# Two projection tiles with 16 extra columns: passes of 512 and 16 columns against passes of 256 and 272

## What is computed

```python
h = concatenate([zeros(PAD), meta, x])            # 16 meta tokens ahead of 512 tokens
hn = rms_norm_2(h, attn_norm_g)
proj = hn @ w_in
aq, ak, av, bq, bkv, iq, ik, iw, gates = split(proj, IN_SPLITS_2)
o_a = sliding_window_sink_attention(aq, ak, av, sinks, bias_a)   # ak: 2 key heads of 64, sliding branch
q = rms_norm_2(bq, q_norm_g) @ w_uq
c_kv = rms_norm_2(bkv, kv_norm_g)                 # 128 shared latent keys and values
o_b = indexed_sparse_mla(q_abs, c_kv, iq, layer_norm(ik), iw, w_uv, bias_b)
mixed = sigmoid(gate_a) * (o_a @ w_branch_a) + sigmoid(gate_b) * (o_b @ w_branch_b)
h = h + mixed @ w_out
```

## Time and profile before

| what | value |
| --- | --- |
| median of 3 runs | 1568.23 us |
| the profiled execution's own time | 1569.13 us |
| its span, first to last instruction | 1567.3 us |
| mean granted TensorE clock | 0.989 |
| TensorE busy | 1520.0 us (97%) |
| VectorE busy | 823.2 us (53%) |
| ScalarE busy | 617.0 us (39%) |
| GpSimd busy | 352.0 us (22%) |

### The profile page before, as it was taken

How to read it: one execution, slowest core, us unless ns; L and a number is a source line. 1 busy time by engine, 2 the same in 40 slices (tenths; PEclk the granted TensorE clock), 3 DMA queues, 4 the chain that set the end, 5 groups by cost and what they waited for, 6 DMA issues and landing times.

```text
span 1567.3 us, 19459 instructions
## 1 busy us (share of the span) xinstructions
PE 1520.0 (97%) x7166; PEld 1206.4 (77%) x7166; DVE 823.2 (53%) x1648; ACT 617.0 (39%) x1119; POOL 352.0 (22%) x364
## 2 busy tenths in 40 slices
PE   7999989999999999999999999999999999999995
PEld 5786656788888888888888778766678888888884
DVE  5556776344445343433446787577365443443444
ACT  6433677322344132322446433566444222221223
POOL 3300455100020000000036534445531210210112
PEclk9999999999999999999999999999999999999998
DMA  5753100433233233333322762312422323333321
GB/s 197 143 150 113 43 15 1 147 95 96 90 97 94 95 94 95 98 104 95 94 89 67 170 175 96 107 48 82 147 95 81 108 94 94 95 102 99 95 81 54
DMA packets 46685, 154.11 MB, mean 98 GB/s; under 512 B 5714, under 2 KB 5906, under 8 KB 46592
## 3 DMA queue, kind: packets, MB, share of 16 engines
q1 hardware_dynamic: 41856, 137.63, 27.8%
q0 software_dynamic: 4736, 15.25, 4.4%
HBM read 142.78 MB, written 9.55 MB: 97 GB/s over the span
## 4 chain that ended last, share of the span: by engine, by line
PE 89%; DVE 5%; ACT 2%; issue 2%; DMA 1%; DVEq 0%; POOL 0%; ACTq 0%; SPq 0%
PE PSA L585 86%; PE PSA L792 2%; DMA WR<-w_in 1%; PE PSA L936 1%; DVE WL L1717 1%; ACT AR L1319 0%; DVE AR L1832 0%; ACT WH L1247 0%; DVE AR L2398 0%; DVE AHL L1925 0%; ACT AHL L1368 0%; DVE AR L1746 0%; DVE AR L2177 0%; DVE ARR L2019 0%; DVE PSA L1755 0%
## 5 line engine op out<-in xcount | busy, mean ns | idle before, releaser
L585 PE MATMUL PSA<-Ah,WH 128*128 128x512 f32 x1072 | 423.7, 395 | 11.9 <-DVE Al L1726 8.1
L585 PE MATMUL PSA<-Ah,WL 128*128 128x512 f32 x1072 | 419.1, 391 | 0.0
L585 PE MATMUL PSA<-Al,WH 128*128 128x512 f32 x1072 | 419.1, 391 | 0.0
L1247 ACT CAST WH<-WR 128x1024 fp32r<-128x1024 f32 (+3 forms) x234 | 241.0, 1031 | 228.7 <-PE PSA L585 217.9
L1717 DVE TENSOR_TENSOR WL<-WR,WH 128x1024 fp32r<-128x1024 f32 (+3 forms) x207 | 255.0, 1232 | 86.1 <-ACT WH L1247 85.9
L585 PEld LDWEIGHTS PSA<-Ah,WH 128*128 128x128 f32 x1072 | 202.4, 189 | 61.5 <-issue 19.0
L585 PEld LDWEIGHTS PSA<-Ah,WL 128*128 128x128 f32 x1072 | 202.4, 189 | 42.8
L585 PEld LDWEIGHTS PSA<-Al,WH 128*128 128x128 f32 x1072 | 202.7, 189 | 41.8 <-issue 0.7
L585 PE MATMUL PSA<-Bh,WH 128*128 128x512 f32 (+1 forms) x592 | 230.5, 390 | 3.9 <-DVE Bl L1996 2.3
L585 PE MATMUL PSA<-Bh,WL 128*128 128x512 f32 (+1 forms) x592 | 229.3, 387 | 0.0
L585 PE MATMUL PSA<-Bl,WH 128*128 128x512 f32 (+1 forms) x584 | 226.7, 388 | 0.0
(11 more groups left out here) (363 smaller groups left out, 1942.1 us busy)
## 6 DMA issues: line engine op xcount, KB each, us to landing
WR<-w_in SPq DMA_DIRECT2D x228, 512.0 KB, 3.5
gt_tmp<-AR SPq DMA_DIRECT2D x16, 256.0 KB, 2.2
WR<-w_in SPq DMA_DIRECT2D x8, 384.0 KB, 3.0
XT<-scr_tmp POOLq DMA_DIRECT2D x8, 264.0 KB, 12.8
XT<-scr_tmp POOLq DMA_DIRECT2D x8, 256.0 KB, 13.6
XT<-xT_in POOLq DMA_DIRECT2D x1, 2048.0 KB, 9.6
x_tmp<-XT POOLq DMA_DIRECT2D x1, 2048.0 KB, 7.7
AHL<-gt_tmp SPq DMA_DIRECT2D x8, 256.0 KB, 4.0
```

Source lines behind the costliest of these rows:

```text
L585: return pe.matmul(o, l, r, start=start, stop=stop)
L1247: ac.copy(WH[p][:, 0:n], WR[j % RAW][:, 0:n]).then_inc(w_hi, 1)
```

## The change

`Ah` and `Al` become 528 columns wide a chunk: the meta tokens' halves stand behind the tokens' in each chunk, and `MH` and `ML` are gone. All other uses of `Ah` and `Al` take columns 0 to 511. For bkv and ak a new function `feat_m` takes each chunk in two passes, columns 0 to 255 and 256 to 527, with the three matmuls of the one and then the three of the other, into two banks of PSUM. The readers follow: VectorE's two instructions on each result take 256 and 272 columns, and the high and low halves of the sliding keys read the tokens as two pieces of 256 from two banks (`in_parts`), the meta tokens as the last 16 columns of the second bank.

```diff
-        with nc.sbuf_tensor("AHL", [128, 16 * T], F) as AHL:
+        with nc.sbuf_tensor("AHL", [128, 16 * TM], F) as AHL:
             pass
-        Ah, Al = sb("Ah", [128, 8, T], R), sb("Al", [128, 8, T], R)
+        Ah, Al = sb("Ah", [128, 8, TM], R), sb("Al", [128, 8, TM], R)
...
-        MH, ML = sb("MH", [128, 8, NM], R), sb("ML", [128, 8, NM], R)
...
-        hA = (lambda k: Ah[:, k, :], lambda k: Al[:, k, :])
+        hA = (lambda k: Ah[:, k, 0:T], lambda k: Al[:, k, 0:T])
+        def in_parts(K):
+            return [x.rearrange("p (a c) -> p a c", a=2) for x in K]
+        hM = [(lambda k, c=c: Ah[:, k, c], lambda k, c=c: Al[:, k, c]) for c in (slice(0, 256), slice(256, TM))]
...
-            def feat(j, src, nk, o, ready=None, om=None, beside=()):
+            def feat(j, src, nk, o, ready=None, beside=()):
...
-                if om is not None:
-                    for k in range(nk):
-                        last = chunk(ws, (lambda k: MH[:, k, :], lambda k: ML[:, k, :]), k, om, nk)
                 last.then_inc(w_mm, 1)
+            def feat_m(j, b):
+                ws = halves_ready(j)
+                for k in range(8):
+                    chunk(ws, hM[0], k, bank(b)[:, 0:256], 8)
+                    last = chunk(ws, hM[1], k, bank(b + 1)[:, 0:272], 8)
+                last.then_inc(w_mm, 1)
...
-                            h1, l1 = (X[:, kx, 128 * a:128 * a + 128] for X in (Ah, Al)) if a < 4 else (MH[:, kx, :], ML[:, kx, :])
+                            h1, l1 = (X[:, kx, 128 * a:128 * a + 128] for X in (Ah, Al)) if a < 4 else (Ah[:, kx, T:TM], Al[:, kx, T:TM])
...
-            feat(tid["bkv", 0], hA, 8, bank(6), om=bank(7)[:, 0:NM])
+            feat_m(tid["bkv", 0], 6)
...
-            feat(tid["ak", 0], hA, 8, bank(2), om=bank(3)[:, 0:NM])
+            feat_m(tid["ak", 0], 2)
...
-                        ac.copy(MH[:, :, :], MGT).then_inc(n_ma.sem, 1)
+                        ac.copy(Ah[:, :, T:TM], MGT).then_inc(n_ma.sem, 1)
...
-            k_high(h_hi, KA, bank(2))
-            k_high(h_hi, KAM, bank(3)[:, 0:NM])
+            k_high(h_hi, in_parts(KA), PSA[:, 2:4, 0:256])
+            k_high(h_hi, KAM, bank(3)[:, 256:272])
...
-                        dv.tensor_tensor(ML[:, :, :], MGT, MH[:, :, :].bitcast(F), ALU.subtract).then_inc(n_md.sem, 1)
+                        dv.tensor_tensor(Al[:, :, T:TM], MGT, Ah[:, :, T:TM].bitcast(F), ALU.subtract).then_inc(n_md.sem, 1)
...
-            dv.tensor_tensor(ckr[:, 0:T], bank(6), rb[:, 0:T], ALU.mult).then_inc(e_d.sem, 1)
-            dv.tensor_tensor(ckr[:, T:TM], bank(7)[:, 0:NM], rb[:, T:TM], ALU.mult).then_inc(e_d.sem, 1)
+            dv.tensor_tensor(ckr[:, 0:256], bank(6)[:, 0:256], rb[:, 0:256], ALU.mult).then_inc(e_d.sem, 1)
+            dv.tensor_tensor(ckr[:, 256:TM], bank(7)[:, 0:272], rb[:, 256:TM], ALU.mult).then_inc(e_d.sem, 1)
...
-            scaled(bank(2), rb[:, 0:T])
-            scaled(bank(3)[:, 0:NM], rb[:, T:TM])
+            scaled(bank(2)[:, 0:256], rb[:, 0:256])
+            scaled(bank(3)[:, 0:272], rb[:, 256:TM])
...
-            k_low(h_lo, KAL, KA, bank(2))
-            k_low(h_lo, KAML, KAM, bank(3)[:, 0:NM])
+            k_low(h_lo, in_parts(KAL), in_parts(KA), PSA[:, 2:4, 0:256])
+            k_low(h_lo, KAML, KAM, bank(3)[:, 256:272])
```

More of the change, by code:

```diff
@@ L1252, in raw_high @@
             def raw_high(nm, k, gain):
-                ac.activation(Ah[:, k, :], x3[:, k, 0:T], ACT.Copy, scale=gain[:, k:k + 1]).then_inc(n_hi.sem, 1)
+                ac.activation(Ah[:, k, 0:T], x3[:, k, 0:T], ACT.Copy, scale=gain[:, k:k + 1]).then_inc(n_hi.sem, 1)
             def square(nm, k, last=True):
@@ L1725, in raw_low @@
                 dv.wait_ge(n_hi.sem, n_hi.at(nm, k))
-                dv.scalar_tensor_tensor(out=Al[:, k, :], in0=x3[:, k, 0:T], scalar=gain[:, k:k + 1], in1=Ah[:, k, :].bitcast(F),
+                dv.scalar_tensor_tensor(out=Al[:, k, 0:T], in0=x3[:, k, 0:T], scalar=gain[:, k:k + 1], in1=Ah[:, k, 0:T].bitcast(F),
                                         op0=ALU.mult, op1=ALU.subtract).then_inc(n_lo.sem, 1)
```

## The result

The changed kernel takes 1583.04 us (median of 7 runs, 1577.73 to 1586.17) where the kernel before took 1572.64 us on the same chip (7 runs, 1563.46 to 1574.57). The ratio is 1.0072, with a 95% interval from 1.0054 to 1.009: slower by 0.7%. The forecast was 1562.0 us, "the same", and its range ended at 1567.0 us, so it was wrong in sign and size. The profiled execution of the changed kernel took 1584.74 us, that of the kernel before 1569.13 us; the spans differ by 15.6 us.

The account below looks back on a forecast made before the run. The prediction took TensorE's own stream, busy 97% of the span, as the bound. From 1569.13 us it took off 4.5 (passes) and 1.7 (clock) for 1562.9, or 1562.0 us as median; range 1559.3 to 1567.0 us.

Parts of the forecast that it names:

- Evictions: VectorE's products, sliding-key reads, meta cast and subtraction, tokmajor's new meta address: together taken as 0, products within 0.1 us either way.
- the loads and some unseen effect of the new addresses: Whole kernel: what would make it slower by over 0.5%, above 1576.1 us; chance 0.05.
- The weight loads come into the open: Rival: weight loads stick out under the two tiles' 96 new matmuls, 16.1 us against 4.5, time 1579.8 us; chance 4%.
- Steps over 130 ns ... would make the prediction wrong in that part: Sign to look for in bkv and ak, where 48 steps of 119 and 126 ns in turns were forecast.
- The passes: In bkv and ak, a pair of matmuls falls from 338.3 to 244.3 ns, saving 4.5 us over both tiles.
- The clock: TensorE's half-speed stretch behind bkv's 16-column matmuls, taken as caused by them, goes too, saving 1.7 us.
- stays or moves elsewhere: Rival: the clock's fall behind bkv remains or comes elsewhere, only the passes count, 1563.7 us; chance 20%.
- A further fall goes as well: Rival: the slow clock from 861.0 to 868.0 us also goes, another 1.7 us, time 1560.3 us; chance 12%.
- The readers of the two tiles: ScalarE's and VectorE's sliding-key halves, reading two pieces of 256: taken as 0, bounded -0.1 to +0.25 us an instruction.
- Does the gain pass?: The gain passes in full behind bkv, with 3 us of cover left; behind ak cover shrinks from 3.3 to 1.0 us.
- gate 9's low half comes late: Rival: behind ak TensorE waits for GpSimd's weights, ak's 2.26 us are lost, time 1566.0 us; chance 8%.
- It doesn't do what it says: Rival: the meta columns are still paid apart and the time stays near 1568.2 us; chance 3%.

Follow-up runs that it names:

- e1: Changed kernel (528-column pitch) with the old passes of 512 and 16 columns: 1587.39 us, ratio 1.011 to the kernel before.
- e2: Changed kernel with a pitch of 576 columns instead of 528 and descriptor space cut from 16 to 12 KB: 1564.94 us, ratio 0.9972 to the kernel before.
- e7: Kernel before with only the weights (raw tiles and halves) shifted by 64 bytes against the 256-byte phase: 1606.17 us, ratio 1.0214.
- e5: Kernel before with 64 unused bytes ahead of the input's halves, so moving operands and weights shift alike: 1572.11 us, ratio 1.0006.
- e11: e1 with a pitch of 576 columns and the smaller descriptor space, so old passes of 512 and 16 columns: 1570.08 us, ratio 0.9991 to the kernel before.
- e12: The kernel of e2 once more, on the same chip as e11: 1565.45 us, ratio 0.9972 to the kernel before.
- e4: e2 with a pitch of 544 columns, putting odd chunks 128 bytes off the phase: 1579.13 us, ratio 1.0065 to the kernel before.
- e3: Kernel before with only GpSimd's descriptor space cut from 16 to 12 KB, the control for e2: 1573.01 us, ratio 1.0018.
- e10: Kernel before with Ah, Al, Bh and Bl shifted 32 bytes off the weights' phase: 1598.85 us, ratio 1.0176.
- e6: Kernel before with Ah, Al, Bh and Bl shifted 64 bytes, the weights and everything behind them kept in phase: 1582.86 us, ratio 1.0077.
- e9: Kernel before with the weights shifted by 128 bytes against the 256-byte phase: 1598.33 us, ratio 1.0172.
- e8: Kernel before with only Al shifted 64 bytes off the phase: 1582.72 us, ratio 1.0064.

## Why the prediction was wrong

**The step that failed** is in "Evictions": "tokmajor takes the 16 meta columns from another address: nothing. No wait, transfer or queue entry is added, removed or moved past another." I looked at the new addresses of the 16 meta columns and not at those that they push away: every chunk of `Ah` and `Al` but the first. 3264 matmuls outside the two tiles read from the moved chunks, six of eight at another phase, and I priced that at nothing without a sentence on it. It measured 15.6 us, two and a half times the 6.2 us of gain in the sum. e1 shows it alone (+18.0 us by medians, +1.1%), e2 shows it gone with the change otherwise intact.

The kernel before held a sign of it, in the very rows that I priced the passes from. The 288-column passes of `tokmajor` move the weights, 1152 bytes a chunk, so the second chunk of each weight tile starts 128 bytes off. The first matmul of the first four chunks, 12 steps each, and of the fifth, TensorE's timeline of the kernel before:

```profile
83.00 0.29 PE L585 MATMUL PSA<-WH,Ah 128*128 128x288 f32 x1
...
84.58 0.29 PE L585 MATMUL PSA<-WH,Ah 128*128 128x288 f32 x1
...
86.18 0.29 PE L585 MATMUL PSA<-WH,Ah 128*128 128x288 f32 x1
...
87.76 0.29 PE L585 MATMUL PSA<-WH,Ah 128*128 128x288 f32 x1
...
89.34 0.30 PE L585 MATMUL PSA<-WH,Ah 128*128 128x288 f32 x1
```

In phase a chunk takes 1.58 us, off phase 1.60: over all eight chunks 131.4 to 131.8 ns a step against 133.2 to 133.5. No row gave the price for 512 columns, where all projection steps were in phase; but a bound was within reach. I bounded the two-piece reads of eight small instructions from both sides, and not the new addresses of 3264 large ones. One nanosecond on each of 3264 steps is 3.3 us, over half of the gain that I forecast. The chance of 5% for slower, "the loads and some unseen effect of the new addresses", was far too low for that.

**The rival on the slower side** named the weight loads, and the wrong place for them. "The weight loads come into the open" looked at what of a load sticks out under the 96 new passes, at 1579.8 us. (It took 168 ns a load, busy time over count; the single records say 0.19 us, with which its 16.1 us would be 18.2.) There nothing sticks out: they cost 118 and 124.5 ns, on the line of the 288-column ones. But its words "Steps over 130 ns ... would make the prediction wrong in that part" looked only into the two tiles. On the 512-column steps, whose 227 ns had seemed to be the stream's alone, a mere shift of the weights costs 6.3 ns (e7). That the load itself is what they pay for fits this, and isn't shown.

The Trainium skill (TensorE: Matmul & The Clock Gate, Step-by-step: what each phase is for) has TensorE read through two independent ports and says "Loading the next tile's weights doesn't steal SBUF read bandwidth from the running matmul". The trace of e7 speaks against it: 233.3 against 227.0 ns with only the weights' addresses changed, while e5, with all shifted alike, has 227.0. Had I doubted it, the rival would have had the whole stream for its place.

**The passes** (4.5 us forecast): right. Steps of 118 and 124.5 ns where 118.8 and 125.5 were forecast, a pair 242.5 ns for 244.3, 4.7 us in the steps, 4.6 us between e11 and e12. (At the pitch of 576 the pair is at the forecast 244.3 ns; the 272-column pass is 1.8 ns faster at 528, so the price of a phase in the table below holds for 512 columns only.) The formula that the prediction set against its sum is given by the Trainium skill (TensorE: Matmul & The Clock Gate, Back-to-back issue gap) for an isolated matmul, with other figures for a stream of loads and matmuls. So it was no rule against the change; no run here has an isolated matmul.

**The clock** (1.7 us forecast, "I take the fall as caused by it"): right in that the fall in the earlier trace rows is gone, about half right as a rule, and the gain didn't arrive in this execution, where 6.8 us more at the lower level cost some 3.4 us. Over all profiled executions of kernels with 16-column stretches, the clock fell to the lower level (1.2 GHz) within seven steps of the stretch in 10 of 20 cases behind the two tiles, five of ten behind bkv and five of ten behind ak; behind the 256- and 272-column passes in 0 of 8 (the changed kernel, e2, e4, e12). The windows of e1, whose thin stretch lies at 850.4 to 852.9 us, show one that fell:

```profile
843.00:853.00 10.00, 10.00 (x57) 8.57 (x55) 8.00 (x8) 6.39 (x10) 9.74 (x8) 1.00 0.26 66
853.00:856.40 3.40, 3.40 (x10) 2.73 (x10) 3.33 (x3) 3.13 (x5) 3.19 (x2) 0.52 0.31 120
```

Full speed through the stretch, half of it right behind, with TensorE busy for the whole of both windows. So the term was one of chance for each of two places: half of 1.7 us, twice, is 1.7 us on the mean. "At most one of the two tiles paid" was this execution's luck: in e1 and e3 both paid. In e1's windows TensorE has no idle gap ahead of the fall.

A third stretch of 24 16-column matmuls, in the second attention, is left in every kernel. Behind it the clock fell within 1.4 us in 6 of 14 executions, the changed kernel's among them. Its windows, with the stretch at 1007.5 to 1010.0 us:

```profile
1007.00:1010.00 3.00, 3.00 (x28) 2.95 (x28) 1.28 (x7) 2.52 (x6) 1.00 (x4) 1.00 0.49 124
1010.00:1013.40 3.40, 3.40 (x15) 3.11 (x15) 2.15 (x12) 1.74 (x6) 1.25 (x3) 0.54 0.77 278
```

That falls come at all is shown; that thin matmuls bring them rests on 16 of 34 against 0 of 8, which is little. And the falls vary more from one execution to the next than the term is large: e2 and e12 are the same kernel, TensorE was at the lower level for 6.8 us ahead of its last matmul in the one and 37.5 in the other, and the spans are 1560.4 and 1570.0 us.

**The rivals on the clock.** The fall behind bkv didn't stay, but others came elsewhere, so "stays or moves elsewhere" came in part. "A further fall goes as well" came too: the one at 861 to 868 us isn't there, and behind the same wait, still 1.04 us and now ending at 867.5 us, the clock is at 1.00 (first row). In its place stands one at 921.5 us, right behind the wait that grew (second row, and below):

```profile
868.00:872.00 4.00, 4.00 (x22) 3.17 (x19) 2.58 (x2) 1.11 (x2) 4.00 (x3) 1.00 0.02 4
...
921.00:924.80 3.80, 3.40 (x10) 2.56 (x11) 3.42 (x5) 3.17 (x8) 3.11 (x2) 0.57 0.75 250
```

**The readers of the two tiles**, also in "Evictions" (0 forecast): right. ScalarE's four high halves of the sliding keys take 2.45 us as in the earlier trace rows, now in two pieces each. Timeline of the changed kernel behind ak: TensorE's first matmul of gate 8, which follows ak's last, then VectorE, ScalarE and GpSimd:

```profile
934.86 0.39 PE L590 MATMUL PSA<-Ah,WH 128*128 128x512 f32 x1
...
935.06 0.78 DVE L1765 TENSOR_TENSOR PSA<-PSA,AR 128x256 f32<-128x256 f32 x2 [1.16 <-PE PSA L590]
...
935.88 2.45 ACT L1322 ACTIVATE Bh<-PSA 64x512 fp32r<-64x512 f32 x4 [5.10 <-DVE PSA L1765]
...
939.04 1.03 ACT L1257 CAST WH<-WR 128x1024 fp32r<-128x1024 f32 x1
...
940.15 4.77 POOL L2427 TENSOR_TENSOR WL<-WR,WH 128x1024 fp32r<-128x1024 f32 x2 [6.88 <-ACT WH L1257]
```

**Does the gain pass?** Yes, at both places. Behind ak the forecast had VectorE busy and the cover shrinking to 1.0 us. In the changed kernel everything comes later by what the stream has lost, VectorE has caught up and waits 1.16 us for the product, and the first low half of gate 9 is ready at 940.15 + 4.77 / 2 = 942.5 us, against its use two tiles behind 934.86, at 946.0: 3.5 us of cover. The rival "gate 9's low half comes late" didn't happen. Behind bkv the forecast left 3 us of VectorE's 7.08 us, and 3.45 are left; TensorE's wait for the products of bq is 1.04 us as before:

```profile
865.40 0.69 DVE L2298 COPY AR<-PSA 128x512 f32<-128x512 f32 x1 [3.45 <-PE PSA L1137]
...
867.52 1.26 PE L590 MATMUL PSA<-AR 64*128 64x512 f32 x8 [1.04 <-DVE AR L2302]
```

One wait grew that I hadn't named. TensorE's list of waits (us in total, times, longest) has 3.3 us for ScalarE at L1632, against 1.1 before, and 9.5 instead of 8.1 us for the loading of `Al`:

```profile
PE PSA L590 <- DVE Al L1736: 9.5, 2, 8.0
...
PE PSA L590 <- ACT AR L1632: 3.3, 1, 3.3
```

ScalarE's cast of a weight block ahead of it waited 7.03 us for its DMA, 4.69 before. Why that load came later I haven't settled; it is at most 2.2 of the 15.7 us, and the clock's fall at 921.5 us comes right behind the wait.

**"It doesn't do what it says"** didn't happen either: the passes are as the diff has them.

## What to carry to other kernels

When a change alters a buffer's pitch or base, list every instruction that streams it, not only those that the change names, and multiply their count by one nanosecond before calling it nothing. Keep the moving operand and the weights of 512-column fp32r matmuls at the same phase modulo 256 bytes, in every chunk: here a pitch of 576 columns instead of 528 turns 0.7% slower into 0.3% faster. To see such a cost, divide the distance between two matmuls some fifty steps apart by the number of steps, since a single record's duration (0.39 us in both) hides it; the mean over a group of a thousand shows it, 398 against 391 ns.

## What the runs showed of the hardware

I hadn't expected that the addresses of a 512-column fp32r matmul's operands set its step at all. By the distance of the moving operand from the stationary one, modulo 256 bytes; in the last three rows the distance changes from step to step or chunk to chunk:

| distance | step, ns | kernel |
|---|---|---|
| 0 | 227.0 | before, e2, e3, e5, e11, e12 |
| +32 bytes | 233.3 | e10 |
| +64 | 229.0 | e6; e7 where weights move (228.9) |
| +128 | 232.5 | e9 |
| -64 | 233.3 | e7; e6 where weights move |
| -32 | 233.3 | e10 where weights move |
| 0 and +64 in turns | 232.0 | e8 (`Al` only) |
| 0 and +128 by chunk | 232.0 | e4 |
| 0, 64, 128, 192 by chunk | 231.8 | changed kernel, e1 |

At most the step is 2.8% longer (233.3 / 227.0). That the stream and the load meet in a shared part of the memory fits all of these, but which part, and why +64 is cheaper than -64, no run shows. Operands that alternate are slow on the steps that are in phase themselves at least in part because the stream takes three to seven steps to settle (e4 and the changed kernel); what settles there, no run shows either. A run with other weights' pitches, or with one weight load left out, would be the next to make, and wasn't made.

The second thing is the floor of a matmul with its own load: 16 columns take 111.5 ns, and in 16 of 34 stretches of 24 of them the clock fell within 1.5 us behind, in e1 with no idle time ahead of it.
